# Second attention: query blocks 1 and 0 in wider steps, 22 steps in place of 32

## The reference, cut to what matters

```
s = einsum('bgrqd,bgrqmd->...', qb, kg)            # selected branch
p_slc = masked_softmax(s - slopes * dist, dist >= 0)
o_slc = p_slc @ vg
s = einsum('bgrqd,bsgd->bgrqs', qb, kw)            # window branch
p_win = masked_softmax(s - slopes * dist_i, mask)
o_win = p_win @ vw
o = gb[..., 0:1] * o_cmp + gb[..., 1:2] * o_slc + gb[..., 2:3] * o_win
```

## Time and profile before

| what | us |
|---|---|
| median of 3 runs | 1850.04 |
| lowest and highest run | 1847.5 and 1853.62 |
| span of the profiled execution | 1849.1 |
| PE busy in it | 1686.1 (91%) |
| DVE busy in it | 814.0 (44%) |
| ACT busy in it | 592.5 (32%) |

### The profile page before, as it was taken

The page is one execution under the profiler, slowest core; times in us unless marked ns, Lnnn a source line. Parts: engine busy times, 40 slices in busy tenths (PEclk is TensorE's granted clock), DMA queues, the critical chain, the costliest instruction groups (busy, mean ns, idle before and its releaser), DMA issues.

```text
span 1849.1 us, 20755 instructions
## 1 busy us (share of the span) xinstructions
PE 1686.1 (91%) x8326; PEld 1123.8 (61%) x8326; DVE 814.0 (44%) x1355; ACT 592.5 (32%) x1058; POOL 121.2 (7%) x133
## 2 busy tenths in 40 slices
PE   6999899988999977999888898999888999999999
PEld 3886567557777753333332233787545678888887
DVE  4655754576433440112111112547567544444444
ACT  4444553664523331001010000531544542222221
POOL 0102111112000001000000000000100001010100
PEclk9999899998999988999999999999999899999999
DMA  9421102123512569999999999343400122222301
GB/s 344 123 69 56 60 1 69 46 93 136 182 43 96 224 255 359 423 424 425 424 424 424 424 425 413 113 139 92 133 1 1 46 91 91 92 92 91 107 30 46
DMA packets 92290, 329.42 MB, mean 178 GB/s; under 512 B 6868, under 2 KB 21860, under 8 KB 67620
## 3 DMA queue, kind: packets, MB, share of 16 engines
q1 hardware_dynamic: 86048, 315.80, 44.1%
q10 hardware_dynamic: 4324, 6.60, 1.1%
q0 software_dynamic: 1824, 5.70, 0.9%
HBM read 322.83 MB, written 4.20 MB: 177 GB/s over the span
## 4 chain that ended last, share of the span: by engine, by line
PE 66%; DMA 14%; DVE 10%; ACT 6%; issue 2%; ACTq 0%; POOL 0%; SPq 0%; DVEq 0%
PE PS L808 22%; PE PS L951 10%; PE PS L1199 9%; DMA ring<-in_w_exp_gate_dram 5%; DMA room<-in_w_exp_up_dram 4%; PE PS L473 3%; DMA ring<-in_w_exp_up_dram 3%; PE PS L469 3%; PE PS L762 2%; PE PS L684 2%; PE PS L1024 2%; PE PS L640 2%; PE PS L962 2%; PE PS L834 1%; DMA xt<-in_ctx_dram 1%
## 5 line engine op out<-in xcount | busy, mean ns | idle before, releaser
L1968 DVE TENSOR_TENSOR wR<-ring,wR 128x1024 fp32r<-128x1024 f32 (+2 forms) x134 | 151.4, 1130 | 212.1 <-ACT wR L1314 212.0
L1314 ACT CAST wR<-ring 128x1024 fp32r<-128x1024 f32 (+2 forms) x134 | 129.9, 970 | 190.3 <-PE PS L1199 115.5
L808 PE MATMUL PS<-xR,wR 128*128 128x512 f32 x768 | 175.6, 389 | 0.9 <-DVE wR L1968 0.9
L1199 PE MATMUL PS<-wR,hR 128*128 128x512 f32 x768 | 175.2, 389 | 0.0
L951 PE MATMUL PS<-room,xeT 128*64 128x512 f32 x528 | 146.6, 594 | 18.6 <-DMA room<-in_w_exp_up_dram 10.1
L808 PEld LDWEIGHTS PS<-xR,wR 128*128 128x128 f32 x768 | 144.0, 188 | 31.1 <-issue 1.3
L1199 PEld LDWEIGHTS PS<-wR,hR 128*128 128x128 f32 x768 | 144.1, 188 | 29.9
L951 PE MATMUL PS<-ring,xeT 128*64 128x512 f32 x480 | 135.2, 605 | 20.0 <-DMA ring<-in_w_exp_up_dram 9.2
L808 PE MATMUL PS<-hR,wR 128*128 128x512 f32 x528 | 124.2, 396 | 4.5 <-DVE xT L2521 2.0
L808 PEld LDWEIGHTS PS<-hR,wR 128*128 128x128 f32 x528 | 100.1, 191 | 29.4 <-issue 5.0
L951 PEld LDWEIGHTS PS<-room,xeT 128*64 128x64 f32 x528 | 46.9, 137 | 97.5 <-issue 97.5
(11 more groups left out here) (510 smaller groups left out, 2780.5 us busy)
## 6 DMA issues: line engine op xcount, KB each, us to landing
room<-in_w_exp_gate_dram SPq DMA_DIRECT2D x33, 1024.0 KB, 26.1
room<-in_w_exp_up_dram SPq DMA_DIRECT2D x33, 1024.0 KB, 26.1
room<-in_w_exp_down_dram SPq DMA_DIRECT2D x33, 1024.0 KB, 26.8
ring<-in_w_exp_gate_dram SPq DMA_DIRECT2D x30, 1024.0 KB, 27.1
ring<-in_w_exp_up_dram SPq DMA_DIRECT2D x30, 1024.0 KB, 26.3
ring<-in_w_exp_down_dram SPq DMA_DIRECT2D x30, 1024.0 KB, 26.5
ring<-in_w_mod_dram SPq DMA_DIRECT2D x12, 2048.0 KB, 9.2
ring<-in_w_in_dram SPq DMA_DIRECT2D x10, 2048.0 KB, 9.6
```

The costliest lines, as they stand in the source:

```text
L808: mm = T.matmul(b, o[s][:, k, :], x(t, k), start=(k == ks[0] and j == 0), stop=(k == ks[-1] and j == 2))
L1199: mm = T.matmul(down[m], uR[:, r % 2, s, k, 128 * i:128 * i + 128], o[t][:, 0, 512 * q:512 * q + 512], start=(k + j == 0), stop=(k == 3 an ...
L1314: A.copy(parts(wR, chunks, n)[0], W.view(unit)[:, ks, cs]).then_inc(act_hi.sem, act_hi.up(key))
L1968: V.tensor_tensor(lo, W.view(unit)[:, ks, cs], hi.bitcast(F32), ALU.subtract) \
```

## The change

The list of steps takes two head pairs together in block 1 and all four in block 0. Blocks 3 and 2 keep their 8 steps each, block 1 has 4 of four heads and 256 keys, block 0 has 2 of eight heads and 128 keys: 22 steps. A wide step fills both of its two score banks (1024 columns), and each turning of a group fills one bank (512 columns). The maximum of a wide step is one instruction over 1024 columns, the exponentials stay one for each head, and the scaling becomes one TENSOR_TENSOR over 1024 columns with the factors broadcast. The pieces of the compressed branch get an index table: those of block 1 stand at 16, 17, 18, 19, 20 (17, 18, 19, 21, 22 before), those of block 0 at 21, 21, 22, 22, 23 (25, 26, 27, 29, 30 before). The four probability buffers swap places.

```
...
-    cp, st2, cst = m10.take("cp", [128, 8, 32]), m10.take("st2", [128, 4, 3, 2]), m10.take("cst", [128, 3, 8])
-    p2 = [q2[:, 0:2, :], q2[:, 2:4, :], p2b[:, 0], p2b[:, 1]]
+    cp, st2, cst = m10.take("cp", [128, 8, 32]), m10.take("st2", [128, 4, 3, 8]), m10.take("cst", [128, 3, 8])
+    p2 = [p2b[:, 0], p2b[:, 1], q2[:, 0:2, :], q2[:, 2:4, :]]
...
             def scores(m):
-                i, j, v = sel_steps[m]
+                i, js, v = sel_steps[m]
                 nk = 128 * (i + 1)
                 b = four.take(T, ("s2", m), act_sel["e", m], 2)
-                for g in range(2):
-                    gs = slice(64 * g, 64 * g + 64)
-                    T.matmul(b[:, 512 * g:512 * g + nk], q2T[gs, j, 128 * i:128 * i + 128], kT2[gs, v, 0:nk],
-                             start=True, stop=False)
-                for g in range(2):
-                    mm = T.matmul(b[:, 512 * g:512 * g + nk], slopes[:, 4 * g + j, :], distR[:, 512 - nk:512],
-                                  start=False, stop=True)
+                for j in js:
+                    at = nk * (j - js[0])
+                    for g in range(2):
+                        gs = slice(64 * g, 64 * g + 64)
+                        T.matmul(b[:, 512 * g + at:512 * g + at + nk], q2T[gs, j, 128 * i:128 * i + 128], kT2[gs, v, 0:nk],
+                                 start=True, stop=False)
+                    for g in range(2):
+                        mm = T.matmul(b[:, 512 * g + at:512 * g + at + nk], slopes[:, 4 * g + j, :], distR[:, 512 - nk:512],
+                                      start=False, stop=True)
                 mm.then_inc(pe_sel.sem, pe_sel.up(("s", m)))
...
                 T.wait_ge(*dve_sel["sc", m])
                 for g in range(2):
                     b = pool.take(T, ("pT2", m, g), (dve_sel if v * g else act_sel)["pT", m, g])
-                    for c in range(i + 1):
+                    for c in range(len(js) * (i + 1)):
                         mm = turn(b[:, 128 * c:128 * c + 128], p2[m % 4][:, g, 128 * c:128 * c + 128])
...
+    def turned2(m, g):
+
+        i, js, v = sel_steps[m]
+        to, b = pT2[v][:, 0:i + 1, g, js[0]:js[-1] + 1, :], bank(("pT2", m, g))[:, 0:128 * len(js) * (i + 1)]
+        if len(js) == 1:
+            return to[:, :, 0, :], b.rearrange("p (c q) -> p c q", q=128)
+        if i == 0:
+            return to[:, 0], b.rearrange("p (j q) -> p j q", q=128)
+        return to.rearrange("p c j q -> p j c q"), b.rearrange("p (j c q) -> p j c q", c=i + 1, q=128)
+
     def select_order(scores, compress1, compress2, compress3, c_scores, c_exp, c_norm, c_turn, c_put, drain, turn2, values2,
                      square2):
 
-        for m in range(36):
-            if m < 32:
+        pieces = {3: (3, 4, 5, 7, 8), 2: (9, 10, 11, 13, 14), 1: (16, 17, 18, 19, 20), 0: (21, 21, 22, 22, 23)}
+        n_steps = len(sel_steps)
+        ends = list(last_of.values())
+        for m in range(n_steps + 4):
+            if m < n_steps:
                 scores(m)
             if m < 3:
                 (compress1, compress2, compress3)[m]()
-            if m >= 3 and (m - 3) % 8 == 7:
+            if m - 3 in ends:
                 values2(m - 3)
-            if 2 <= m < 34:
+            if 2 <= m < n_steps + 2:
                 turn2(m - 2)
             for n, step in enumerate((c_scores, c_exp, c_norm, c_turn, c_put)):
-                at = (3, 4, 5, 7, 8)[n], (9, 10, 11, 13, 14)[n]
-                if m == at[0] or m >= at[1] and (m - at[1]) % 8 == 0 and m < 32:
-                    step(3 if m == at[0] else 3 - m // 8)
-            if m in (32, 33):
-                drain(m)
-            if m >= 4 and (m - 4) % 8 == 7:
+                for i in range(3, -1, -1):
+                    if pieces[i][n] == m:
+                        step(i)
+            if m in (n_steps, n_steps + 1):
+                drain(m - n_steps)
+            if m - 4 in ends:
                 square2(sel_steps[m - 4][0])
...
                 for g in range(2):
-                    c = A.activation(p2[m % 4][:, g, 0:nk], bank(("s2", m))[:, 512 * g:512 * g + nk], ACT.Exp,
-                                     bias=st2[:, m % 4, 0, g:g + 1], accum_out=st2[:, m % 4, 1, g:g + 1])
+                    for j in range(len(js)):
+                        x = len(js) * g + j
+                        c = A.activation(p2[m % 4][:, g, nk * j:nk * j + nk],
+                                         bank(("s2", m))[:, 512 * g + nk * j:512 * g + nk * j + nk], ACT.Exp,
+                                         bias=st2[:, m % 4, 0, x:x + 1], accum_out=st2[:, m % 4, 1, x:x + 1])
...
-                    A.copy(pT2[v][:, 0:i + 1, g, j, :],
-                           bank(("pT2", m, g))[:, 0:128 * i + 128].rearrange("p (c q) -> p c q", q=128)) \
-                        .then_inc(s.sem, s.up(("pT", m, g)))
+                    A.copy(*turned2(m, g)).then_inc(s.sem, s.up(("pT", m, g)))
...
-                if m == 32:
-                    A.wait_ge(*pe_sel["s", 31])
+                if m == 0:
+                    A.wait_ge(*pe_sel["s", len(sel_steps) - 1])
                     A.wait_ge(*dve_sel["conv"])
                     conv_hi((4, 5))
-                    A.wait_ge(*pe_sel["pT", 29, 1])
+                    A.wait_ge(*pe_sel["pT", len(sel_steps) - 3, 1])
...
+                nk, nj = 128 * (i + 1), len(js)
+                b = bank(("s2", m))
+                b = b.rearrange("p (g x) -> p g x", g=2)[:, :, 0:nk] if nj == 1 else b.rearrange("p (x k) -> p x k", k=nk)
                 V.wait_ge(*pe_sel["s", m])
-                V.tensor_reduce(st2[:, m % 4, 0, :], bank(("s2", m)).rearrange("p (g x) -> p g x", g=2)[:, :, 0:nk], AX,
-                                ALU.max, negate=True).then_inc(s.sem, s.up(("max", m)))
+                V.tensor_reduce(st2[:, m % 4, 0, 0:2 * nj], b, AX, ALU.max, negate=True).then_inc(s.sem, s.up(("max", m)))
                 if m:
                     scale(m - 1)
 
             def scale(m):
-                i, j, v = sel_steps[m]
-                nk = 128 * (i + 1)
-                r = st2[:, m % 4, 2, :]
+                i, js, v = sel_steps[m]
+                nk, nj = 128 * (i + 1), len(js)
+                r = st2[:, m % 4, 2, 0:2 * nj]
+                gates = gat[:, i, :].rearrange("p (g j b) -> p g j b", g=2, b=3)[:, :, js[0]:js[-1] + 1, 1 + v]
                 V.wait_ge(*act_sel["e", m])
-                V.reciprocal(r, st2[:, m % 4, 1, :]).then_inc(s.sem, s.up())
+                V.reciprocal(r, st2[:, m % 4, 1, 0:2 * nj]).then_inc(s.sem, s.up())
                 V.wait_ge(*s.last)
-                V.tensor_tensor(r, r, gat[:, i, :].rearrange("p (g j b) -> p g j b", g=2, b=3)[:, :, j, 1 + v], ALU.mult) \
+                V.tensor_tensor(r.rearrange("p (g j) -> p g j", g=2), r.rearrange("p (g j) -> p g j", g=2), gates, ALU.mult) \
                     .then_inc(s.sem, s.up())
                 V.wait_ge(*s.last)
-                for g in range(2):
-                    p = p2[m % 4][:, g, 0:nk]
-                    V.tensor_scalar(p, p, r[:, g:g + 1], None, ALU.mult).then_inc(s.sem, s.up())
+                if nj == 1:
+                    for g in range(2):
+                        p = p2[m % 4][:, g, 0:nk]
+                        V.tensor_scalar(p, p, r[:, g:g + 1], None, ALU.mult).then_inc(s.sem, s.up())
+                else:
+                    p = p2[m % 4].rearrange("p g (j k) -> p (g j) k", k=nk)
+                    V.tensor_tensor(p, p, r.unsqueeze(2).broadcast_to([128, 2 * nj, nk]), ALU.mult).then_inc(s.sem, s.up())
                 s.also(("sc", m))
...
-                if m == 30:
-                    scale(31)
+                i, js, v = sel_steps[m]
+                if m == len(sel_steps) - 2:
+                    scale(m + 1)
                 if v:
-                    if i < 3 and j == 0:
+                    if i < 3 and js[0] == 0:
                         V.wait_ge(*pe_sel["o", i + 1])
                     V.wait_ge(*pe_sel["pT", m, 1])
-                    V.tensor_copy(pT2[1][:, 0:i + 1, 1, j, :],
-                                  bank(("pT2", m, 1))[:, 0:128 * i + 128].rearrange("p (c q) -> p c q", q=128)) \
-                        .then_inc(s.sem, s.up(("pT", m, 1)))
+                    V.tensor_copy(*turned2(m, 1)).then_inc(s.sem, s.up(("pT", m, 1)))
...
-    sel_steps = [(i, j, v) for i in range(3, -1, -1) for j in range(4) for v in range(2)]
+    sel_steps = [(i, js, v) for i, together in ((3, 1), (2, 1), (1, 2), (0, 4))
+                 for js in (range(j, j + together) for j in range(0, 4, together)) for v in range(2)]
+    last_of = {step[0]: m for m, step in enumerate(sel_steps)}
```

More of the change, by code:

```diff
@@ L1775, in scores @@
             def scores(m):
-                nk = 128 * (sel_steps[m][0] + 1)
+                i, js, _ = sel_steps[m]
+                nk = 128 * (i + 1)
                 if m >= 4:
@@ L1806, in turn2 @@
             def turn2(m):
-                i, j, v = sel_steps[m]
```

(7 more changed lines are left out.)

## The result

The changed kernel takes 1865.5 us (median of 5 runs, 1864.72 to 1866.88) against 1853.62 (5 runs, 1847.5 to 1858.03) before: ratio 1.0074, 95% interval 1.0056 to 1.0092. The forecast was 1857 with a range up to 1863. The direction was right. The forecast was +6.6 us and the medians differ by 11.9, nearly twice that, and the time lies outside the range.

What follows compares the result with a forecast made beforehand. No engine is full; chains through DVE and ACT against PE work beside them bound the stretch. Stalls +9.4, full clock -6.35, clock fall +3.6 give +6.6 us on 1850.04: 1856.6, rounded to 1857; range 1847.5 to 1863.

Steps and rivals of the forecast that it cites:

- Where: Difference lies between block 1's first scores and `wo2`, which becomes about 65 us long; blocks 3 and 2 unchanged.
- the stretch: The part from block 1's first scores to `wo2`, 58.8 us before, the only part the change touches.
- What DVE saves: Maxima, reciprocals, gate and scaling: 7.5 us less DVE work, some 5.5 with overlap; by itself no gain.
- The stalls: Six PE stalls from step 19 to the end, with 0.5 for the root: 17.8 us against 8.4, +9.4.
- The third: Steps 21 and 22: `values2` of block 1 waits for ACT's copy behind eight exponentials, stall 2.9 us.
- the last: The end: the last square waits behind DVE's remaining work and ACT's inverse root, stall 3.2 us.
- The clock: Granted clock falls from step 22 on, slowing `c_turn(0)`, the last turning, total and values: +3.6 us.
- the first stall: Step 19: `square2` of block 2 waits for a bank that ACT empties behind the exponentials, 1.9 us.
- the sum: Over the stretch: stalls +9.4 less 6.35 for full clock gives +3.0, plus 3.6 for the clock: +6.6 us.
- clock down early: Rival, chance 0.15: clock falls already behind the 3.5 us stall at step 20; about +11.6 us, 1861.6.
- the two at step 19 and 20: Bank waits of `square2` of block 2, 1.9 us, and of half the turning of step 18, 3.5 us.
- the four others: `values2` of block 1, 2.9; `c_turn(0)`, 3.9; `square2(1)`, 1.9; the end, 3.2 us.

Runs made afterwards that it cites:

- e7: The change with block 0 in pairs of head pairs (24 steps) and compressed pieces moved, old probability buffer order; ratio to the kernel before 0.9954.
- e4: The change with one number altered, `c_turn` of block 1 at index 20 in place of 19; ratio to the kernel before 0.9994.
- e5: The change plus 16 matmuls that compute nothing needed, put where PE stalls; ratio to the kernel before 1.0003.
- e9: e7 with `c_turn` of block 1 put back from index 20 to 19; ratio to the kernel before 1.0030.
- e11: e4 with a wide step's scaling as one TENSOR_SCALAR for each head; ratio to the kernel before 1.0006.
- e6: The change's 22 steps with compressed pieces at 15, 16, 17, 19, 19 and 20, 20, 21, 22, 23; ratio to the kernel before 1.0016.
- e1: The change with block 0 back to single head pairs (28 steps) and its compressed pieces spread as before; ratio to the kernel before 1.0025.
- e2: The change with block 1 back to single head pairs (26 steps), its pieces as before, block 0's still packed; ratio to the kernel before 1.0034.
- e8: The kernel before, 32 narrow steps, with `c_turn` of blocks 1 and 0 in the index of `c_put` or right before it; ratio 0.9985.
- e3: The kernel before, 32 narrow steps, with only the compressed pieces of blocks 1 and 0 packed close together; ratio 1.0021.

## Why the prediction was right or wrong

- *Where*: right. 13.4 of the 15.1 us of span are in the stretch.
- *What DVE saves*: about right as work (4.5 us of busy time against some 5.5), right as worth nothing in this order; in e7's order wide steps pay.
- *The stalls*: the layout's 1.9, 3.5, 2.9, 3.9, 1.9 and 3.2 us came as 2.07, 3.11, 1.20, 3.95, 1.97 and 0.79. The chains were right. The third and the last are shorter because PE's work beside them ran at half clock and filled them: in e4, with the clock up, the third is 2.77, and the last has 6.6 us of PE work beside it in place of 3.8. In sum 13.7 us of idle time against 17.8.
- *The clock*: the step that failed. "I take it down from step 22 on" priced it at +3.6 us; it fell at step 19, behind the first stall of 2.07 us, stayed low for 27 us and fell twice more. In the terms of the sum: the stalls added 5.3 us where it had 9.4, and PE's work was 58.5 us where at full clock it would be 50.4 - 6.35 = 44.1, so 14.4 where the sum had 3.6. The two errors have opposite signs, and part of the first is the slow work in the stalls' place; e5 puts the clock's price in the stretch at 7.7 us or more. What I had read in the rows was that the clock fell before behind stalls of at most 1.7 us; I used that to say that a fall must come, and then gave it to the longest stalls rather than to the first. The rival *clock down early* had the mechanism, put it one stall too late, and had a price of +11.6 us. That this is so near the measured +11.9 of the medians is in part luck, since it was built on the +9.4 of stalls. It had a chance of 0.15, and a range that ended at 1863 cut it off half way.
- *Which stall matters*: the prediction listed six and treated them alike. The runs with one index moved (e4, e9) show that the two at step 19 and 20 are worth 12.4 and 15.6 us with the clock that falls behind them, and the four others together cost about what the wide steps save: with them e4 stands at 59.8 us against 58.8.
- *A reading*: the view of the earlier trace rows begins at 1384, and one of its three waits for `cpT`, 1.27 us, ends at 1383.81, ahead of the stretch. So DVE is named in 6.2 of the 8.4 us, in seven stalls, not in 7.5 and eight. No term of the sum rests on it.
- *The Trainium skill*: the rule on two-source fp32 operations ("VectorE: DVE Perf Modes", section "Mode 2×_2P — use both read ports for one tensor") holds for each element and was not the point here (e11: 1.66 and 1.14 us in one-source instructions against 1.22). That activity releases the clock ("TensorE: Matmul & The Clock Gate", section "Part 1: The HAM clock gate") agrees with e5, where matmuls without purpose took the granted clock of the stretch from 0.73 to 0.92. e6 does not agree: there the clock stayed at 0.50 for 23.8 us in which the window below shows PE busy all the time, and the measurement decides.

**PE before**, the three longest stalls of its stretch, and the first row behind the fall of the clock:

```profile
1404.27 0.65 PE L469 MATMUL PS<-ident,p2b 128*128 128x128 f32 x4 [1.75 <-DVE p2b L2667]
...
1410.06 0.63 PE L469 MATMUL PS<-ident,q 128*128 128x128 f32 x4 [1.41 <-DVE cpT L2722]
...
1425.96 0.44 PE L469 MATMUL PS<-ident,p2b 128*128 128x128 f32 x2 [1.47 <-DVE p2b L2667]
1426.44 1.07 PE L469 MATMUL PS<-ident,cp 128*32 128x128 f32 x8
1427.45 0.80 PE L1070 MATMUL PS<-kT,q2T 64*128 64x128 f32 x4
```

**Windows at low clock** behind stalls: e6 (2.07 us), e9 (2.07), e1 (2.07), e4 (2.77), e7 (2.54):

```profile
1412.60:1436.40 23.80, 23.80 (x104) 15.72 (x104) 9.65 (x20) 7.55 (x36) 0.00 (x0) 0.50 0.00 0
1410.30:1434.10 23.80, 21.16 (x89) 12.88 (x89) 8.96 (x21) 6.47 (x28) 0.00 (x0) 0.50 0.00 0
1415.70:1432.70 17.00, 14.69 (x61) 8.37 (x63) 7.17 (x19) 3.96 (x15) 0.00 (x0) 0.50 0.00 0
1427.30:1430.60 3.30, 3.30 (x8) 0.93 (x10) 0.00 (x0) 0.00 (x0) 0.00 (x0) 0.50 0.00 0
1433.40:1436.70 3.30, 3.14 (x8) 0.49 (x4) 1.94 (x3) 2.27 (x4) 0.00 (x0) 0.50 0.00 0
```

In all four profiled executions with the 2.07 us stall at `square2(2)` (the change, e1, e6, e9) the clock fell at most 1.7 us after it and stayed low for 17 to 27 us. That it does so in every execution is not shown; the five runs of the change lie within 2.2 us, which speaks for it. The length of a stall doesn't settle the length of the low spell: behind e4's 2.77 us before the values of block 1 and e7's 2.54 before those of block 0 it lasted 3.3 us. Behind e2's 2.17 and e11's 2.75 us, also before the values of block 1, it was 6.7 us. Nor does a stall settle whether the clock falls: the one of 1.75 us left it up in the kernel before, and in e2 and e8 the same stall brought it down for 3.3 us; the one of 1.47 us brought it down in the kernel before and left it up in e7. Why, and what ends a low spell, is open.

## What to carry to other kernels

When buffers are handed out in a ring, count what a piece holds from its take to its release across the places where the ring comes round: here one index, with `c_turn` right before the copy that frees it, was worth all that the change had cost. Wider steps paid here only where the other engines' chain for one step had PE work beside it. And a new stall of 2 us on TensorE is to be priced with a spell at half clock behind it, from the first stall on: in these traces 3 to 7 us long where a block's values came behind the stall, 17 to 27 where `square2` and the 128-column matmuls of the next steps did.

## What was not expected of the hardware

- One stall of 2.07 us was followed by 27 us at a granted clock of 0.50 although PE was busy for 23.0 us of them. Most of what ran there were turnings and scores of 128 columns or less. What kept it low is not tested.
- Matmuls without a use, put into stalls, made the kernel faster: 1.0003 against 1.0074.
- The kernel before ran between 1846.1 and 1861.3 us over all rounds, and untouched blocks 3 and 2 took 63.7 to 71.2 us at mean clocks of 0.97 (e3) and 0.90 (e7). A gain of 0.3% needs many runs here.
